# Moving bias products, first weight loads and the beta weights' split into the input's normalisation, with its tiles written out

## What is computed

```python
h = _rms_norm(x, p['norm_pre_mix'][l])
proj = h @ p['w_in'][l]
a_qkv, b_qkv, z, b_pre, a_pre, gate_a, gate_b = jnp.split(proj, SPLIT_IDX, axis=-1)
...
beta = jax.nn.sigmoid(b_pre.astype(jnp.float32))
g = -jnp.exp(p['a_log'][l]...) * jax.nn.softplus(a_pre... + p['dt_bias'][l]...)
```

## Time and profile before

| | us |
|---|---|
| median of 3 runs | 2455.29 (2455.25 to 2456.33) |
| the profiled execution | 2455.94 |
| its span, first to last instruction | 2454.2 |
| TensorE busy in it | 2260.9 (92%) |
| VectorE busy | 1240.2 (51%) |
| ScalarE busy | 724.6 (30%) |

### The profile page before, as it was taken

One profiled execution on the slowest core, in us unless ns is written; L12 is line 12 of the kernel. 1 busy time (PEld: TensorE's weight loads), 2 busy tenths in 40 slices (PEclk: granted clock), 3 DMA queues, 4 the chain that ended last, 5 costly groups with the idle time before them and its releaser, 6 DMA issues. The chain is left out here.

```text
span 2454.2 us, 36492 instructions
## 1 busy us (share of the span) xinstructions
PE 2260.9 (92%) x14592; PEld 2103.0 (86%) x14592; DVE 1240.2 (51%) x2361; ACT 724.6 (30%) x1620; POOL 65.2 (3%) x76
## 2 busy tenths in 40 slices
PE   5888898699999999999999698897999999889898
PEld 3677787599999999999999698676999999868676
DVE  4123221365676666667666633446666666531243
ACT  4123231323234232332423300454222222231221
POOL 0000000001001010100101000000000000000000
PEclk9989999688999999999999899898999999989999
DMA  4010201441122121312213243521222222151432
GB/s 142 32 65 12 85 12 51 92 104 52 57 58 59 52 83 28 87 58 57 69 46 108 85 134 125 184 87 52 79 82 80 77 77 77 46 171 25 146 116 65
DMA packets 213984, 191.20 MB, mean 78 GB/s; under 512 B 33539, under 2 KB 187172, under 8 KB 213830
## 3 DMA queue, kind: packets, MB, share of 16 engines
q1 hardware_dynamic: 199802, 142.13, 20.0%
q10 hardware_dynamic: 11120, 36.96, 3.8%
q0 software_dynamic: 2944, 10.49, 1.6%
HBM read 138.09 MB, written 51.64 MB: 77 GB/s over the span
## 5 line engine op out<-in xcount | busy, mean ns | idle before, releaser
L265 PE MATMUL bank<-xT_hi,w_lo 128*128 128x344 f32 x1152 | 395.7, 343 | 4.9 <-DVE w_lo L261 4.9
L267 PE MATMUL bank<-xT_hi,w_hi 128*128 128x344 f32 x1152 | 370.0, 321 | 0.0
L266 PE MATMUL bank<-xT_lo,w_hi 128*128 128x344 f32 x1152 | 369.9, 321 | 0.0
L265 PEld LDWEIGHTS bank<-xT_hi,w_lo 128*128 128x128 f32 x1152 | 219.4, 190 | 6.1 <-DVE w_lo L261 5.4
L266 PEld LDWEIGHTS bank<-xT_lo,w_hi 128*128 128x128 f32 x1152 | 219.3, 190 | 0.0
L267 PEld LDWEIGHTS bank<-xT_hi,w_hi 128*128 128x128 f32 x1152 | 218.2, 189 | 0.0
L1093 PE MATMUL bank<-xT_hi,f_hi 128*128 128x258 f32 x704 | 199.6, 283 | 0.0
L1089 PE MATMUL bank<-xT_hi,f_lo 128*128 128x258 f32 x704 | 199.3, 283 | 0.0
L1091 PE MATMUL bank<-xT_lo,f_hi 128*128 128x258 f32 x704 | 199.2, 283 | 0.0
L265 PE MATMUL bank<-fo_wh,fo_sl 128*128 128x512 f32 (+1 forms) x396 | 157.8, 398 | 27.9 <-DVE fo_wl L261 22.9
L266 PE MATMUL bank<-fo_wl,fo_sh 128*128 128x512 f32 (+1 forms) x396 | 156.9, 396 | 0.0
(11 more groups left out here) (407 smaller groups left out, 4947.6 us busy)
## 6 DMA issues: line engine op xcount, KB each, us to landing
w_raw<-in_w_in SPq DMA_DIRECT2D x48, 512.0 KB, 3.9
f_raw<-in_w_ffn_in SPq DMA_DIRECT2D x44, 512.0 KB, 4.9
act_scr<-f_y ACTq DMA_DIRECT2D x22, 516.0 KB, 2.7
fo_sr<-act_scr SPq DMA_DIRECT2D x16, 704.0 KB, 6.7
fo_wr<-in_w_ffn_out SPq DMA_DIRECT2D x22, 512.0 KB, 5.1
gate_scr<-gate ACTq DMA_DIRECT2D x16, 516.0 KB, 3.1
a_kv_raw<-in_w_in SPq DMA_DIRECT2D x3, 2048.0 KB, 9.4
mix_ta<-gate_scr SPq DMA_DIRECT2D x8, 516.0 KB, 4.9
```

What stands on the lines that cost most here:

```text
L265: nc.tensor.matmul(out, stat_lo, mov_hi, start=start, stop=False)
L266: nc.tensor.matmul(out, stat_hi, mov_lo, start=False, stop=False)
L267: return nc.tensor.matmul(out, stat_hi, mov_hi, start=False, stop=stop)
```

## The change

The normalisation's block and the attention block's memory are now set up together, and work of the later block stands inside the earlier one.

- The normalisation's tiles are written out, without the hardware loop, in the same order on each engine. `tiles` calls `beside(t)` behind the last step of tile t.
- The table of ones is set at the start of VectorE's list; the block of its own is gone.
- ScalarE's queue issues the loads of `ident`, of the bias table and of `onehot` before its first statistics. SP issues tile 0's rows before the norm weights.
- VectorE widens the bias table before its first centring. TensorE makes bias products 2t and 2t + 1 behind the turn of tile t (t = 0 to 5), into banks 4 to 7, and VectorE copies them out behind the split of tile t.
- SP issues the four beta loads behind the load of tile 4. ScalarE and VectorE split the beta weights behind tile 6's last step.
- SP issues the loads of the first k/v weights, in two halves, and of the query weights behind the load of tile 8, in the normalisation's block.
- In the attention block ScalarE and VectorE split the k/v weights in two halves, and ScalarE does so before it copies the beta results.

```diff
-                        sp.dma_start(wrow[:], weight.partition_broadcast(P)).then_inc(const, 16)
-                        sp.dma_start(ident[:], a["c_ident"]).then_inc(const, 16)
-                        tiles(sp, load, nothing)
...
+            def tiles(eng, stage, finish, beside):
+
+                def at(t):
+                    return eng, t // 2, t % 2, P if t < NT else NS, t
+
+                stage(*at(0))
+                for t in range(1, NT + 2):
+                    if t <= NT:
+                        stage(*at(t))
+                    finish(*at(t - 1))
+                    beside(t - 1)
...
+                @block.sync
+                def _(sp):
+                    load(sp, 0, 0, P, 0)
+                    sp.dma_start(wrow[:], weight.partition_broadcast(P)).then_inc(const, 16)
+                    for t in range(1, NT + 1):
+                        load(sp, t // 2, t % 2, P if t < NT else NS, t)
+                        if t == BETA - 2:
+                            loads_beside(sp)
+                    loads_last(sp)
+
+                @block.vector
+                def _(v):
+                    def beside(t):
+                        for n in (2 * t, 2 * t + 1):
+                            if n < NG * HA:
+                                bias_copies(v, n)
+                        if t == BETA:
+                            beta_dve(v)
+
+                    start(v, 1, *(e.sem for e in made + lo_done))
+                    nc.vector.memset(stat[:, :, 3:4], EPS).then_inc(eps, 1)
+                    nc.vector.memset(ident_ones[:], 1.0).then_inc(ones_set, 1)
+                    bias_wide(v)
+                    v.wait_ge(const, 16)
+                    tiles(v, center, split, beside)
+                    v.wait_ge(ones_set, 1)
...
+                    start(act, 1, *(e.sem for e in squared))
+                    act.dma_start(ident[:], a["c_ident"]).then_inc(ident_ld, 16)
+                    loads_first(act)
+                    act.wait_ge(eps, 1)
+                    tiles(act, stats, split_hi, beside)
...
+            def products(pe, n):
+                if n == 0:
+                    pe.wait_ge(spread, 1)
+                if n >= 4:
+                    pe.wait_ge(cp, n - 3)
+                nc.tensor.matmul(banks[4 + n % 4][:, :3 * P], wide[:, n], onehot[:, n // HA],
+                                 start=True, stop=True).then_inc(mm, 1)
...
+                def first_loads(sp):
+                    for half, loaded in ((slice(0, 4), kv_first), (slice(4, KT), kv_ld)):
+                        sp.dma_start(kv_raw[:, half], w_in[:, half, Q:Q + KV]).then_inc(loaded, 16)
+                    sp.dma_start(q_raw[:], w_in[:, :, :Q]).then_inc(q_ld, 16)
...
-                    bias_load(sp)
-                    beta_load(sp)
-                    load(0, "kv"); load(0, "q")
                     bias_store(sp)
                     beta_over(sp)
...
+                    act.wait_ge(kv_first, 16)
+                    nc.scalar.activation(kv_hi[:, :4], kv_raw[:, :4], ACT.Copy).then_inc(kv_half, 1)
+                    act.wait_ge(kv_ld, 16)
+                    inc(nc.scalar.activation(kv_hi[:, 4:], kv_raw[:, 4:], ACT.Copy), "kv_hi")
                     beta_act(act)
-                    split_kv(0)
...
-                    bias_copies(v)
-                    beta_dve(v)
-                    split_kv(0)
+                    v.wait_ge(kv_half, 1)
+                    split_lo(v, kv_lo[:, :4], kv_raw[:, :4], kv_hi[:, :4])
+                    wt(v, "kv_hi", 0, 1)
+                    inc(split_lo(v, kv_lo[:, 4:], kv_raw[:, 4:], kv_hi[:, 4:]), "kv_lo")
```

More of the change, by code:

```diff
@@ L390, in over @@
                 eng.wait_ge(ac, 7)
-            return load, pe_first, pe_second, act_first, act_second, dve_first, dve_second, over
[L394 to L400, removed]
+            return load, pe_first, pe_second, act_split, act_first, act_second, dve_split, dve_second, over, (ld, sp_hi, sp_lo)
         att_scr = dram("att_scr", (NG, L, HA * (HD + 2)))
@@ L434, in bias_steps, with load @@
             ld, spread, mm, cp, out = sem("b_ld"), sem("b_spread"), sem("b_mm"), sem("b_cp"), sem("b_out")
[L436 to L439 removed]
+            def load(act):
+                act.dma_start(table[:32], a["rel_bias"]).then_inc(ld, 16)
+                act.dma_start(table[32:33], a["c_ones"][0:1, :NG * HA]).then_inc(ld, 16)
+                act.dma_start(onehot[:], a["c_onehot"]).then_inc(ld, 16)
             def store(sp):
@@ L444, in store, with widen, copies @@
                 sp.wait_ge(out, 16)
-            def products(pe):
-                pe.wait_ge(spread, 1)
-                for n in range(NG * HA):
-                    if n >= 8:
-                        pe.wait_ge(cp, n - 7)
-                    nc.tensor.matmul(banks[n % 8][:, :3 * P], wide[:, n], onehot[:, n // HA],
-                                     start=True, stop=True).then_inc(mm, 1)
-            def copies(v):
+            def products(pe, n):
[5 more added lines that the diff above has]
+                                 start=True, stop=True).then_inc(mm, 1)
+            def widen(v):
                 v.wait_ge(ld, 48)
                 nc.vector.tensor_copy(wide[:], table[:].unsqueeze(2).to_broadcast([33, NG * HA, P])).then_inc(spread, 1)
-                for n in range(NG * HA):
-                    v.wait_ge(mm, n + 1)
-                    nc.vector.tensor_copy(res[:, n], banks[n % 8][:, :3 * P]).then_inc(cp, 1)
+            def copies(v, n):
+                v.wait_ge(mm, n + 1)
+                nc.vector.tensor_copy(res[:, n], banks[4 + n % 4][:, :3 * P]).then_inc(cp, 1)
             def over(eng, stored):
@@ L465, in over, with attention_block @@
                     eng.wait_ge(out, 16)
-            return load, store, products, copies, over
-        def attention_block():
-            used = list(live)
-            with ExitStack() as s, nc.Block() as block:
+            return load, store, products, widen, copies, over, (ld, spread, mm)
+        def attention_block(used):
+            with ExitStack() as s:
                 KV, Q = 2 * HA * HD, HA * HD
@@ L1527, in _ @@
                         tiles_of(v, q, stage, split_weights, finish, turn_in)
[L1529 to L1530 removed]
+        norm_sems = []
+        attention_block(norm_sems)
         for x in norm_sems:
```

205 lines of the change are left out of this document (97 added, 108 removed).

## The result

| | before | after |
|---|---|---|
| median, us | 2455.27 (4 runs, 2454.75 to 2456.33) | 2431.30 (4 runs, 2430.55 to 2431.99) |
| profiled execution, us | 2455.94 | 2431.99 |
| its span, us | 2454.2 | 2430.2 |

The ratio is 0.9902, with a 95% interval of 0.9885 to 0.9919. The kernel is 24.0 us faster; 26.9 was forecast. The time lies in the stated range of 2421 to 2435.

The account below looks back on a forecast made before the run. TensorE bounds the kernel, seldom idle outside its opening chain of stages. First k/v matmul 24.1 us earlier plus 2.8 from the clock make 26.9, taking 2455.94 to 2429.0, or 2428.4 beside the median; range 2421 to 2435.

Parts of the forecast that it names:

- first transposes: Start of TensorE's work on tile 0, after widening and centring: about 9.4 us instead of 9.92, a gain of 0.5.
- six tiles: Tiles 0 to 5 with two bias products each: TensorE sets the pace at 4.37 us a tile, 26.2 in all.
- tail to the last split: Tiles 6 to 8 with the added beta and memset instructions at full price: 8.0 us, normalisation ending at 43.6.
- to the first beta matmul: Between the blocks only one barrier of 0.49 us remains, so beta matmuls begin at 44.1 instead of 59.66.
- beta matmuls: TensorE's beta stretch in the attention block takes 13.22 us as before, with some at the low clock level.
- first k/v matmul: Begins at 57.3 us instead of 81.39, directly behind the beta matmuls, the weight split being ready by 51.3.
- won by k/v matmuls at the higher clock: Without the idle 8.5 us before them, the first 14 k/v matmuls take 3.1 us instead of 5.90: 2.8 gained.
- the rest: Everything behind the k/v matmuls is shifted by 27 us with its durations kept.
- later bound of 12: Start: onehot lands at 12 us if served last, instead of 7.0; widening then ends at 13, costing 4.5.
- Lockstep: Rival: TensorE waits for the centring in each of six tiles, 6.7 us instead of 4.37, giving 2442; chance 0.05.
- rival of a released clock: Opening's clock goes to 2.4 GHz: tiles at 3.5 us, beta matmuls in 10.8, total 2422; chance 0.12.
- Given back: Rival: behind the opening, shifted clock falls meet other pauses and change the time by 11 us, 2439 (or 2418); 0.05.

Follow-up runs that it names:

- widening later: Changed kernel with VectorE's widening copy of the bias table behind its first centring instead of in front of it; median 2428.12 us.
- More switches: Changed kernel with the first bias product of each tile between the two halves of its transposes; median 2434.07 us.
- two-pass: Changed kernel, widening behind the first centring, each bias product in two passes from high and low rounded table parts and a rounded onehot; 2422.52 us, ratio 0.9872.
- products back: Changed kernel with the bias products and their copies put back behind the normalisation, in front of the beta matmuls; median 2435.68 us.
- split behind: Changed kernel with ScalarE's first k/v split put back behind its copies of the beta results, still in halves; median 2436.79 us.
- loads late: Changed kernel with the first k/v and query weight loads issued in the attention block instead of behind tile 8's load; median 2429.95 us.

## Why the prediction came out as it did

The mechanism was right: the opening's stages overlap, TensorE becomes the pace of tiles 0 to 5, and the k/v split is hidden. What was off are sizes of the sum. In the table "off" is how much later than forecast the kernel is by that term.

| term of the sum | forecast | measured | off |
|---|---|---|---|
| first transposes | 9.4 | 11.01 | +1.6 |
| six tiles | 26.2 | 28.50 | +2.3 |
| tail to the last split | 8.0 | 7.32 | -0.7 |
| to the first beta matmul | 0.5 | 0.33 | -0.2 |
| beta matmuls | 13.2 | 13.65 | +0.4 |
| first k/v matmul | 57.3 | 60.81 | +3.5 |
| won by k/v matmuls at the higher clock | 2.8 | 2.86 | -0.1 |
| the rest | 0 | -0.6 | -0.6 |

The 2.86 is from the first k/v matmul to the beta transposes, 54.74 before (136.13 - 81.39) and 51.88 after. Together the terms are 2.9 off, 2431.3 instead of 2428.4. Errors of both signs met in it; the late ones alone come to 4.3. The range had no term for the tiles, and this was the largest error. That the rests of these two executions lie within 0.6 us is luck, since those of all the kernels go from 2313.8 to 2319.7.

**The start.** "So I take 7.0" for onehot, an issue that ends at 3.6 and 3.4 to land. The issue ended at 2.62, since ScalarE's queue did not wait for the table load (0.75 to 2.03) and began at 0.85; but onehot was there at 8.77, 6.15 us after the end of its issue, against 2.1 in the quiet stretch. The two errors are in opposite directions, and the landing was the larger. The later bound of 12 covered it. The experiment with the widening later shows that this wait held the first centring by 2.2 us (6.56 against 8.77), and that with the copy itself it was the whole loss at the start.

**The tiles.** "1.75 + 2.62 = 4.37" adds the two kinds of work as if the second followed the first at the usual spacing. It does not: 0.19 and 0.29 are lost when TensorE goes from transposes to products and back. (Eight transposes at 256 / 1.2 GHz are 1.71, and 1.90 passed; four instructions at 0.64 are 2.56, and 2.85 passed.) More switches shows that it is a price of the change, not of the tile. A tile is 0.38 above the sum and not 0.48, because the forecast counted transposes and products 0.10 too long. VectorE was not the pace, and no wait in tiles 0 to 5 was TensorE's. Lockstep is refuted.

**The tail.** Full price for the four beta instructions (1.0) was too much; 0.3 of it reached the end. VectorE's two (0.46) fell into its wait for ScalarE's statistics of the last tile, which was 0.59 before and is now:

```profile
44.03 1.27 DVE L199 SCALAR_TENSOR_TENSOR normed<-rows,stat,wrow 8x1024 f32<-8x1024 f32 x1 [0.84 <-ACT stat L185]
```

**The clock.** The rival of a released clock is refuted: TensorE was busy for 28.50 us on end, and its products still took 0.64 an instruction, the 1.2 GHz level by the same working as before. The two-pass instructions at 0.32 for one pass of 384 columns say the same. The column of the granted clock shows 1.00 in both kernels' tiles and products, but the kernel with the products back has a recorded change early, and its rows settle it. These are the transposes of two tiles, and then the column over one stretch of transposes and over its products:

```profile
17.43 1.09 PE L215 MATMUL bank<-ident,normed 128*128 128x128 f32 x8 [2.96 <-DVE normed L199]
20.00 1.97 PE L215 MATMUL bank<-ident,normed 128*128 128x128 f32 x8 [1.47 <-DVE normed L199]
...
17.40:18.60 1.20, 1.09 (x8) 0.86 (x8) 1.17 (x2) 1.14 (x5) 0.00 (x0) 0.98 0.38 27
38.48:54.11 15.63, 15.63 (x25) 7.80 (x25) 6.13 (x11) 4.95 (x3) 0.00 (x0) 0.50 0.20 62
```

Eight transposes take 1.09 at the 2.4 GHz level and 1.97 at the 1.2 GHz level, and 1.97 is what they take in the tiles of before and after. The 12 products take 15.63 at a recorded 0.50, as they do before at a recorded 1.00. So the opening runs at the low level in both kernels, as the prediction took it, and the column does not tell before its first change. The level can rise in the opening all the same. Here one tile (17.43) ran at the high one, behind 16 transposes of 3.65 us in all and a pause of 2.96. In split behind, loads late, widening later and more switches it rose behind the 16 transposes of tiles 6 and 7: the eight small ones of the last tile take 0.66 there, against 1.02 in the changed kernel, and the low level is back with the first beta matmuls. It did not rise behind every such 16 (the kernel before at 9.92, the changed one at 39.51), and in no kernel while products stood between the tiles.

The beta matmuls began at 0.29 each and went to 0.16 at 52.3, 5.1 us after their start, where it was 3.7 before. These 1.4 us more at half speed cost some 0.6; the forecast's 13.2 held 0.2 of it already, the overlapped end of the last matmul, and the 0.4 is left. The rule of the Trainium skill, TensorE: Matmul & The Clock Gate, Part 1, that sustained activity releases the clock, does not agree with the products in either kernel (15.72 and 28.50 us busy on end at the low level); the beta matmuls, which rose, agree with it.

**The split of the gain.** It goes by steps in the table of instants. The first beta matmul is 5.6 earlier with the products back behind the normalisation (59.66 to 54.11): that is onehot's early load, the missing block and the beta weights' early split, for whose low part TensorE waited 0.94 before. It is 7.0 earlier again with the products in the tiles (54.11 to 47.16). From the first beta to the first k/v matmul it was 21.73 and is 13.65, 8.1 less. The wait in it was 8.50, is 6.87 with the halves behind the beta copies, and 0 with them in front: 1.6 are the halves and 6.9 their place, and 0.4 comes back because the beta matmuls were longer at the low level. Together 20.6 (81.39 to 60.81), and 2.86 from the clock: 23.4. The k/v loads' early place earns nothing on its own. Writing out the tiles gains 0.44 a pair against the earlier trace rows, but in the changed kernel nothing, because TensorE's 4.75 a tile is above either pace.

**Given back.** No gain was lost behind the opening. But the rest differs by up to 6 us between the profiled executions, which have the same instructions there; the five runs of one kernel (loads late) lie 11 us apart in their totals, so it need not be the kernels that make this difference. One place shows a part of it. These are the stretches behind TensorE's pause before the output projection, in the changed kernel and then in the kernel with the loads late:

```profile
1518.00:1523.00 5.00, 4.59 (x11) 3.66 (x12) 4.00 (x5) 3.44 (x4) 0.00 (x0) 0.50 0.83 276
1523.00:1528.00 5.00, 5.00 (x23) 4.11 (x22) 3.40 (x3) 2.51 (x3) 0.00 (x0) 0.95 0.81 301
```

```profile
1518.00:1523.00 5.00, 5.00 (x16) 3.92 (x15) 3.91 (x4) 2.78 (x3) 0.00 (x0) 0.65 0.78 279
1523.00:1528.00 5.00, 5.00 (x24) 4.14 (x23) 3.00 (x4) 3.19 (x3) 0.00 (x0) 1.00 0.74 253
```

In the first TensorE begins at 1518.40 and its matmuls follow each other at 0.43 until 1523.5, then at 0.23: 5.1 us at the low level (granted clock 0.50). In the second it begins at 1517.50 and changes at 1521.4, after 3.9 us (0.65 over a stretch that holds both levels). At half speed 1.2 us more cost about 0.6. So how long TensorE works at the low level behind a pause differs between executions with the same instructions there; that this makes up the whole difference of the two rests, 2317.5 and 2314.6, was not followed further and stays open.

## What to carry to other kernels

When work is moved into the gaps of another stage, write down what the moved-to engine then needs for one round, with a price for each change between kinds of work, and compare it with the pace of the round: what is above comes back. A load that was quick in a quiet stretch is not quick in front of the first big transfers, so the instruction that waits for it must not stand ahead of the first link of the chain. For edits of a few us in a kernel of 2.4 ms, read the instants of the stage that was changed; the total moves by as much as that for other reasons.

## What the runs showed that I had not expected

- TensorE kept its low level through 28.5 us of transposes and products without a pause, and through 15.7 of products alone. Beta matmuls came up to the high level 3.1 to 6.0 us after they began, with the same 72 instructions in all kernels; what stands in front of them does not sort the values.
- The level rose for a moment behind 16 transposes in a row in five of the kernels, and not in the others that had them.
- The column of the granted clock stood at 1.00 up to its first change, while the spacing of matmuls said half. In the kernel with the products back, where it had changed before, it read 0.50 over the same products.
- A change from transposes to 33-row products and back costs 0.46 to 0.49 us at the low level, and as much with the rounded one-pass products.
- A load in the hardware loop comes about 0.3 us later than the same load written out.
